# The state-space core of a hybrid mixer, placed between the units of the projection that follows it

## The chip, the core and the metric

The kernel runs on one core of one Trainium2 chip. The core has five engines that run their own queues of instructions: TensorE (PE; matrix products, results in the eight banks of PSUM), VectorE (DVE), ScalarE (ACT), GpSimd (POOL) and SyncE (SP, which here only issues transfers from HBM). They wait for each other by semaphores. The metric is the device time of one execution in microseconds (us), the median of several; lower is better. All data are float32.

## The reference, cut to what matters

Two transformer blocks run on 256 tokens of width 1024. The first block's mixer projects the normed tokens `h` with `w_in` and has two branches. The change touches the SSD branch's core and the GDN branch's projection, which are independent of each other until both outputs are concatenated:

```python
proj = h @ w_in
# GDN branch: 3072 columns q, k, v; 1024 columns gate z
qkv = silu(causal_dwconv(gdn_qkv, gdn_conv_w))          # 4 taps
q = l2norm(q_heads) * (128 ** -0.5); k = l2norm(k_heads)
o = gated_delta_rule_chunked(q, k, v, beta, g)          # the GDN core
gdn_out = rmsnorm(o, gdn_norm_g) * silu(gdn_z)
# SSD branch: xs (16 heads of 64), bm and cm (2 groups of 128), dt
xbc = silu(causal_dwconv(ssd_xbc, ssd_conv_w) + ssd_conv_b)
y = ssd_chunked(xs, dt, ssd_a_log, bm, cm) + ssd_d[:, None] * xs
y = y * silu(ssd_z)
ssd_out = rmsnorm(y.reshape(.., 2, 512), ssd_norm_g)
return concatenate([gdn_out, ssd_out], axis=-1) @ w_out
```

Behind the mixer come a mixture of 32 experts, and a second block with its own mixer and 32 experts.

## The kernel before

**Stages.** The program is a chain of `nc.Block()`s. In each block every engine has its own list of instructions, and at the end of a block all engines meet before the next begins. The blocks around the change are, in order: (1) modulation and first norm; (2) the SSD projection (three weight chunks for x, B, C, two for the gate, a narrow one for dt), with its convolution; (3) the SSD core; (4) the GDN projection; (5) the GDN core; (6) the late modulation, `w_out` and the router; then the experts.

**The ring of weights.** `ring` holds `SLOTS` = 6 slots of 4096 floats for each of 128 partitions, 2 MB each. Chunk n goes to slot n % 6. `load` (lines 168 to 180) runs on SP: it waits until the slot's previous chunk has been multiplied and starts the transfer. `take` makes TensorE wait for the arrival. The other large memory is `arena`, 25600 floats a partition, whose places are given out by hand for each block.

**Block 3, the SSD core** (lines 492 to 594) goes over the two token tiles t = 0, 1 of 128 tokens, and uses all eight banks of PSUM. For each tile ScalarE repeats the decays of 16 heads along 128 columns (`abc`, line 531), TensorE multiplies them by a triangle of ones (line 506; decay rows), and in the same go makes the group products and the transposes of B and x (lines 511 to 515). VectorE subtracts, giving exponents of 16 head matrices (line 554), ScalarE exponentiates them, VectorE copies B, C-B products and x out of PSUM and forms the operands (lines 559 to 569), TensorE multiplies them (line 519, 16 products of 64 columns; line 523 the state of tile 0, or line 525 the read of it in tile 1), and VectorE forms the output, its gate, its sum of squares and its norm (lines 577 to 594). Tile 1 needs the state of tile 0. Scratch lies in `arena`.

**Block 4, the GDN projection** (lines 614 to 686). The 24 units u are blocks of 128 output channels by 256 tokens, eight products of 256 columns each (line 635), written to PSUM bank u % 6. VectorE does the four taps of the convolution out of the bank (`conv`, lines 368 and 372), ScalarE the Silu (line 661), GpSimd the squares of the 16 units of q and k (line 624). From unit 16 on, one length product of 512 columns follows each unit (line 645; eight in all, in banks 6 and 7), copied out by ScalarE (line 665). Then come four gate units of 16 products of 512 columns (line 653), beside which ScalarE takes the logarithm and exponential of the lengths, and VectorE scales q and k.

**Block 5, the GDN core**: SP starts the transfer of the norm weight `gng` (line 731); VectorE's list begins with a wait for it (`dve.wait_ge(s_gn, 16)`), before its first operation (line 848).

**Order of the queues.** Nothing is reordered by a planner: an engine's list is the order in the source. `then_inc` raises a semaphore when an instruction is done, `wait_ge` holds the engine and all that is queued behind it. `vv(...)` is a VectorE instruction followed by a wait for its own end.

Of the kernel before, what the change touches and what calls it, by code (L numbers as in the profile page):

```python
# [11 lines left out]
P = 128  # L12
D = 1024
T = 2
# [27 lines left out]
def program(nc, a, out):  # L42
# [103 lines left out]
    class Ring:  # L146
# [3 lines left out]
        def __init__(self, name, slots=SLOTS):  # L150
            self.slots = slots
            self.full = [sem(f"{name}_slot{s}_full") for s in range(slots)]
            self.arrivals = []
            self.chunks, self.sent, self.used = [], 0, 0

        def add(self, src, shape, released):


            n = len(self.chunks)
            before = self.arrivals[n - self.slots] if n >= self.slots else 0  # L160
            self.arrivals.append(before + (32 if isinstance(src, list) else 16))
            self.chunks.append((src, shape, released))

        def last_uses(self):

            return [(n % self.slots, *self.chunks[n][2]) for n in range(len(self.chunks) - self.slots, len(self.chunks))]

        def load(self, sp, upto):
            while self.sent < min(upto, len(self.chunks)):
                n = self.sent  # L170
                src, (k, w), _ = self.chunks[n]
                s = n % self.slots
                if n >= self.slots:
                    sp.wait_ge(*self.chunks[n - self.slots][2])
                if isinstance(src, list):
                    for i in range(2):
                        sp.dma_start(slot(s, k, w)[64 * i:64 * i + 64], src[i]).then_inc(self.full[s], 16)
                else:
                    sp.dma_start(slot(s, k, w), src).then_inc(self.full[s], 16)
                self.sent += 1  # L180

        def take(self, pe):
            n = self.used
            pe.wait_ge(self.full[n % self.slots], self.arrivals[n])
            self.used += 1
            _, (k, w), _ = self.chunks[n]
            return slot(n % self.slots, k, w)
# [6 lines left out]
    for j in range(4):  # L194
        ra.add(cols(ada_w, 512 * j), (KD, 512), (s_ada, j + 1))
    for j in range(3):
        ra.add(cols(w_in, C_XBC + 512 * j), (KD, 512), (s_unit, 4 * j + 4))
    for j in range(2):
        ra.add(cols(w_in, C_SZ + 512 * j), (KD, 512), (s_unit, 12 + 2 * j + 2))
    for j in range(6):  # L200
        ra.add(cols(w_in, 512 * j), (KD, 512), (s_gunit, 4 * j + 4))
    for j in range(2):
        ra.add(cols(w_in, C_GZ + 512 * j), (KD, 512), (s_gunit, 24 + 2 * j + 2))
    for j in range(4, 12):
        ra.add(cols(ada_w, 512 * j), (KD, 512), (s_ada, j + 1))
    s_wout = sem("w_out_chunk_multiplied")
    for n in range(2):
        for k in range(2):
            ra.add(a["w_out"][0][1024 * k:1024 * k + 1024, 512 * n:512 * n + 512]
                   .rearrange("(k p) n -> p k n", p=P), (KD, 512), (s_wout, 2 * n + k + 1))  # L210
# [43 lines left out]
    with nc.Block() as block:  # L254
        @block.sync
        def _(sp):
# [14 lines left out]
            ra.load(sp, 4 + SLOTS)  # L271
# [89 lines left out]
    def conv(dve, n, nbanks, dst, tap0, bias0, ready, taken, taps):  # L361

        for u in range(n):
            dve.wait_ge(ready, u + 1)
            src = ps[:, u % nbanks, 0:T * P]
            w = [convw[:, tap0 + k * taps + u:tap0 + k * taps + u + 1] for k in range(4)]
            if bias0 is None:
                vv(V.tensor_scalar(dst(u), src, w[3], None, ALU.mult))
            else:
                vv(V.tensor_scalar(dst(u), src, w[3], convw[:, bias0 + u:bias0 + u + 1], ALU.mult, ALU.add))  # L370
            for s in (1, 2, 3):
                ins = V.scalar_tensor_tensor(dst(u)[:, s:T * P], src[:, 0:T * P - s], w[3 - s], dst(u)[:, s:T * P],
                                             ALU.mult, ALU.add)
                if s < 3:
                    vv(ins)
                else:
                    ins.then_inc(taken, 1)

    with nc.Block() as block:
        @block.sync  # L380
        def _(sp):
            ra.load(sp, 9 + SLOTS)
# [63 lines left out]
        def _(dve):  # L446
            conv(dve, 12, 8, lambda u: xbcT[:, u, :], 96, 144, s_unit, s_conv, 12)
# [15 lines left out]
    x_tok = ar(6400, D)  # L463
    b_tok = ar(7424, 2, P)
    xdt = ar(7680, D)
    xde = ar(8704, D)
    state = ar(9728, 2, 512)
    yb = ar(10752, D)
    abc = ar(17408, SH, P)
    dmat = ar(19456, SH, P)  # L470
    cbT = ar(21632, 2, P)
    ysq = ar(21888, D)
    sng = ar(22912, D)
# [3 lines left out]
    atot = small[:, 392:408]  # L477
# [5 lines left out]
    s_tr = sem("ssd_transposes")  # L483
# [5 lines left out]
    s_y3t = sem("ssd_products_taken")  # L489
    s_var3, s_root3 = sem("ssd_squares_summed"), sem("ssd_roots_ready")  # L490

    with nc.Block() as block:  # L492
        @block.sync
        def _(sp):
            sp.dma_start(sng, row_everywhere(a["ssd_norm_g"][0])).then_inc(s_p3, 16)

        @block.tensor
        def _(pe):
            for t in range(T):
                tok = slice(t * P, (t + 1) * P)  # L500
                pe.wait_ge(s_abc, t + 1)
                if t:
                    pe.wait_ge(s_y3t, 1)
                    pe.wait_ge(s_st, 1)
                for h in range(SH):
                    last = M.matmul(ps[:, h // 4, (h % 4) * P:(h % 4 + 1) * P], abc[:, h, :], tri_le[:, :])
                M.matmul(ps[:, 4, 0:SH], tri_le[:, :], dec[:, t, 8:24])
                last = M.matmul(ps[:, 4, 16:16 + SH], ones[:, :], dec[:, t, 8:24])
                last.then_inc(s_row, 1)
                for g in range(2):  # L510
                    M.matmul(ps[:, 5, g * P:(g + 1) * P], xbcT[:, 8 + g, tok], xbcT[:, 10 + g, tok])
                for g in range(2):
                    last = M.transpose(ps[:, 5, (2 + g) * P:(3 + g) * P], xbcT[:, 8 + g, tok], ident[:, :])
                for k in range(KD):
                    last = M.transpose(ps[:, 6 + k // 4, (k % 4) * P:(k % 4 + 1) * P], xbcT[:, k, tok], ident[:, :])
                last.then_inc(s_tr, 1)
                pe.wait_ge(s_m3, 2 * t + 2)
                for h in range(SH):
                    last = M.matmul(ps[:, h // 8, (h % 8) * SP_:(h % 8 + 1) * SP_], abc[:, h, :],
                                    xdt[:, h * SP_:(h + 1) * SP_])  # L520
                for g in range(2):
                    if t == 0:
                        last = M.matmul(ps[:, 2 + g, :], b_tok[:, g, :], xde[:, g * 512:(g + 1) * 512])
                    else:
                        last = M.matmul(ps[:, 2 + g, :], xbcT[:, 10 + g, tok], state[:, g, :])
                last.then_inc(s_y3, 2)

        @block.scalar
        def _(act):
            def repeat_decays(t):  # L530
                A.activation(abc, bcast(dec[:, t, 8:24], P), ACT.Copy).then_inc(s_abc, 1)
            repeat_decays(0)
            for t in range(T):
                act.wait_ge(s_dx, 3 * t + 1)
                A.activation(eac, acum, ACT.Exp).then_inc(s_de, 1)
                A.activation(edec, edec, ACT.Exp).then_inc(s_de, 1)
                for q in range(2):
                    act.wait_ge(s_dx, 3 * t + 2 + q)
                    A.activation(dmat[:, 8 * q:8 * q + 8, :], dmat[:, 8 * q:8 * q + 8, :], ACT.Exp).then_inc(s_de, 1)
                if t == 0:  # L540
                    act.wait_ge(s_y3, 2)
                    repeat_decays(1)
                    A.activation(state, banks(2, 2, 2, 512), ACT.Copy).then_inc(s_st, 1)
                act.wait_ge(s_var3, t + 1)
                A.activation(gss, gss, ACT.Sqrt, bias=eps_t, scale=1.0 / 512).then_inc(s_root3, 1)

        @block.vector
        def _(dve):
            for t in range(T):
                dve.wait_ge(s_row, t + 1)  # L550
                vv(V.tensor_copy(acum, ps[:, 4, 0:SH]))
                V.tensor_tensor(edec, ps[:, 4, 16:16 + SH], acum, ALU.subtract).then_inc(s_dx, 1)
                for h in range(SH):
                    ins = V.scalar_tensor_tensor(dmat[:, h, :], ps[:, h // 4, (h % 4) * P:(h % 4 + 1) * P],
                                                 acum[:, h:h + 1], neg_u, ALU.subtract, ALU.add)
                    if h % 8 == 7:
# [1983 lines left out]
```

## Time and profile before

| what | value |
|---|---|
| median of 3 runs | 2439.54 us (2438.66 to 2441.5) |
| profiled execution, its own time | 2437.12 us |
| its span | 2435.4 us |
| TensorE busy | 2124.4 us, 87% |
| VectorE, ScalarE, GpSimd busy | 569.1, 371.3, 82.0 us |
| granted TensorE clock, mean | 0.934 |

The span runs from the first to the last instruction of the profiled execution; 1.7 us of its own time lie outside. TensorE's busy time is that of its matrix products with modelled ends. The time before is the median; durations in the argument come from the one profiled execution.

### The profile page before, as it was taken

How to read it: one execution, taken by the hardware profiler on the slowest of the kernel's cores; microseconds unless marked ns; L12 is line 12 of the kernel's file. 1: busy time of each engine (PE TensorE's matmuls, PEld its weight loads, DVE VectorE, ACT ScalarE, POOL GpSimd, SP SyncE). 2: the span in 40 equal slices, each digit the busy share in tenths (PEclk: the TensorE clock that was granted, in tenths of full speed). 3: DMA queues.
4: the chain of work that ended last, by engine and by line, in shares of the span. 5: the costliest groups of instructions: out<-in, count | busy, mean ns of one | idle time of the engine just before them, and what ended most of it. 6: DMA issues, size and time to landing. Idle time of an engine off the chain costs nothing. (4 is left out here: it accounts for less than half of the span.)

```text
span 2435.4 us, 25005 instructions
## 1 busy us (share of the span) xinstructions
PE 2124.4 (87%) x10073; PEld 1099.0 (45%) x10073; DVE 569.1 (23%) x1204; ACT 371.3 (15%) x633; POOL 82.0 (3%) x151
## 2 busy tenths in 40 slices
PE   4957977796999999999999999699957699999997
PEld 1746846733444443333333333255544344444443
DVE  1345535413121111111111111322152300010001
ACT  2130132111000100000100000113230111111111
POOL 1000012200000000000000000100030000000000
PEclk7977988997899999999999999899958799999999
DMA  9511320093699999999999999734314179999995
GB/s 338 193 43 45 135 98 1 1 343 124 258 428 428 429 428 429 428 429 428 429 428 429 427 429 428 291 124 158 104 40 149 69 325 426 429 427 429 428 429 232
DMA packets 98733, 708.58 MB, mean 291 GB/s; under 512 B 12291, under 2 KB 17885, under 8 KB 61565
## 3 DMA queue, kind: packets, MB, share of 16 engines
q1 hardware_dynamic: 98684, 707.92, 70.9%
q8 instruction: 33, 0.54, 0.1%
q14 instruction: 16, 0.12, 0.0%
HBM read 706.85 MB, written 1.05 MB: 291 GB/s over the span
## 5 line engine op out<-in xcount | busy, mean ns | idle before, releaser
L1272 PE MATMUL ps<-ring,arena 128*64 128x512 f32 x2048 | 451.9, 594 | 28.1 <-DMA ring<-in_moe_w_gu 28.1
L1272 PEld LDWEIGHTS ps<-ring,arena 128*64 128x64 f32 x2048 | 161.3, 137 | 312.4 <-issue 247.9
L1294 PE MATMUL ps<-ring,arena 128*64 128x512 f32 x1024 | 226.8, 594 | 19.6 <-issue 19.6
L2401 PE MATMUL ps<-ring,arena 128*64 128x512 f32 x1024 | 224.9, 593 | 6.9 <-DMA ring<-in_w_up 5.4
L1294 PEld LDWEIGHTS ps<-ring,arena 128*64 128x64 f32 x1024 | 84.6, 137 | 141.2 <-issue 141.2
L2401 PEld LDWEIGHTS ps<-ring,arena 128*64 128x64 f32 x1024 | 78.2, 137 | 150.4 <-issue 150.4
L1609 PE MATMUL ps<-ring 128*128 128x512 f32 (+1 forms) x320 | 139.0, 586 | 1.2 <-DVE ring L1879 0.9
L2422 PE MATMUL ps<-ring,arena 128*64 128x512 f32 x512 | 113.4, 595 | 0.0
L1337 DVE TENSOR_SCALAR arena<-arena 128x256 f32<-128x256 f32 x33 | 11.7, 354 | 380.6 <-PE ps L1272 380.5
L1364 DVE TENSOR_SCALAR arena<-ps 128x512 f32<-128x512 f32 x32 | 22.1, 691 | 332.4 <-PE ps L1272 332.4
L1318 ACT ACTIVATE arena<-arena 128x512 f32<-128x512 f32 x32 | 20.2, 630 | 522.2 <-DVE arena L1364 522.2
L635 PE MATMUL ps<-arena,ring 128*128 128x256 f32 x384 | 86.4, 386 | 12.4 <-PEq L492 12.4
L1609 PEld LDWEIGHTS ps<-ring 128*128 128x128 f32 x320 | 60.3, 193 | 69.1 <-issue 66.2
L2461 DVE TENSOR_SCALAR arena<-iota_row,arena 128x64 f32<-128x64 f32 x68 | 12.6, 249 | 329.0 <-PE ps L2401 327.9
L635 PEld LDWEIGHTS ps<-arena,ring 128*128 128x128 f32 x384 | 74.4, 194 | 27.1 <-issue 17.0
L1235 PEld LDWEIGHTS ps<-arena 128*128 128x128 f32 x544 | 64.9, 196 | 27.5 <-issue 27.5
L1235 PE MATMUL ps<-arena 128*128 128x128 f32 x544 | 71.2, 286 | 0.0
L2379 PEld LDWEIGHTS ps<-arena 128*128 128x128 f32 x544 | 62.1, 192 | 13.5 <-issue 13.5
L1242 PE MATMUL ps<-arena 64*128 64x512 f32 x264 | 65.6, 615 | 0.8 <-ACT arena L1325 0.8
L2422 PEld LDWEIGHTS ps<-ring,arena 128*64 128x64 f32 x512 | 35.3, 137 | 66.7 <-issue 66.7
L2379 PE MATMUL ps<-arena 128*128 128x128 f32 x544 | 65.1, 278 | 0.0
L2386 PE MATMUL ps<-arena 128*128 128x512 f32 x136 | 61.3, 593 | 0.7 <-ACT arena L2454 0.7
(516 smaller groups left out, 2154.7 us busy)
## 6 DMA issues: line engine op xcount, KB each, us to landing
ring<-in_moe_w_gu SPq DMA_DIRECT2D x128, 2048.0 KB, 24.1
ring<-in_moe_w_down SPq DMA_DIRECT2D x64, 2048.0 KB, 21.4
ring<-in_w_down SPq DMA_DIRECT2D x32, 2048.0 KB, 12.2
ring<-in_w_gate SPq DMA_DIRECT2D x32, 2048.0 KB, 14.9
ring<-in_w_up SPq DMA_DIRECT2D x32, 2048.0 KB, 17.2
ring<-in_w_in SPq DMA_DIRECT2D x22, 2048.0 KB, 10.7
ring<-in_ada_w SPq DMA_DIRECT2D x12, 2048.0 KB, 9.5
ring<-in_w_out SPq DMA_DIRECT2D x6, 2048.0 KB, 19.2
```

The lines of the kernel that those rows point to most:

```text
L635: last = M.matmul(ps[:, u % 6, 0:T * P], w[:, k, c * P:(c + 1) * P], hT[:, k, :], start=(k == 0), stop=(k == KD - 1))
L1235: last = M.matmul(ps[:, bank, k4 * P:(k4 + 1) * P], x_tok[:, t, k * P:(k + 1) * P], onehot[:, t, :], start=(t == 0), stop=(t == T - 1))
L1242: last = M.matmul(ps[:, 2 * t + j, :], GT[halves[j], t, :], y2[halves[j], :], start=False, stop=False, skip_group_check=True)
L1272: last = M.matmul(ps[halves[j], 4 + which, :], xgT[buf][:, k, CAP * ee:CAP * ee + CAP], w[:, k2, at:at + 512], start=False, stop=(k == KD ...
L1294: last = M.matmul(ps[halves[j], 6, :], yT[:, k % KH, halves[k // KH]], w[:, k % KH, 512 * j:512 * j + 512], start=(k == 0), stop=(k == 2 * ...
L1318: A.activation(sg, tg, ACT.Sigmoid, scale=1.702).then_inc(s_sig, 1)
L1364: V.tensor_scalar(tg, ps[:, 4, :], 7.0, None, ALU.min).then_inc(s_g, 1)
L1609: last = M.matmul(ps[:, bank, 0:n], uT[:, k, t * P:(t + 1) * P], w[:, k, :], start=(k == 0), stop=(k == KD - 1))
L2379: last = M.matmul(ps[:, 6 + k // 4, (k % 4) * P:(k % 4 + 1) * P], x_tok[:, t, k * P:(k + 1) * P], onehot[:, t, :], start=(t == 0), stop=(t ...
L2386: M.matmul(ps[:, 2 * t + d, :], GT[:, t, :], y2[:, d, :], start=False, stop=False, skip_group_check=True)
L2401: last = M.matmul(ps[halves[j], 4 + which, :], xgT[:, k, halves[j]], w[j][:, k, :], start=(k == 0), stop=(k == KD - 1))
L2422: last = M.matmul(ps[halves[j], (4, 7)[d], :], yT[:, k, halves[j]], w[j][:, k, 512 * d:512 * (d + 1)], start=(k == 0), stop=(k == KH - 1))
```

## The change

Blocks 3 and 4 become one. Each step of the SSD core is a small function, and is called behind a given GDN unit, on each of the three engines that take part:

| behind unit (tile 0, tile 1) | TensorE | ScalarE | VectorE |
|---|---|---|---|
| 0, 8 | decay rows of heads 0 to 7, group products | exponentials of them | exponents of heads 0 to 7 |
| 1, 9 | | | B and C-B products taken |
| 2, 10 | decay rows of heads 8 to 15 | exponentials of them | exponents of heads 8 to 15 |
| 3, 11 | transposes of x | x taken | |
| 4, 12 | | | operands |
| 6, 14 | products | (6 only) decays repeated, state taken | outputs, gated |
| 7, 15 | | squares, root | norm |

Further parts of it:

- GDN units use `GB` = 3 banks (u % 3) and bank 3 takes the length products; banks 4 to 7 are the SSD core's, and later the gate units'.
- A length product follows every second unit from 5 to 19, not every unit from 16 to 23. It is copied out by ScalarE behind units 6, 8, ..., 20. Squares have four pairs of places (`sqT`), reused.
- x is taken out of PSUM by ScalarE, and the sums of squares of the output are made by ScalarE (`Square` with `accum_out`, two of 512 columns); VectorE did both.
- The SSD core's scratch lies in ring slots 3, 4 and 5. In this block the ring has only slots 0 to 2: each chunk now names its slot. Of the loads, chunks 12 to 16 (the last three of q, k, v and both gate chunks) are issued in the merged block, and the six chunks of `ada_w` that were issued in block 4 are issued at the start of block 5, behind `gng`. Chunk 9 is issued in block 2, no longer in block 1. In block 6 the last chunks and the experts' first loads have other slot numbers.

```diff
+    abc, dmat = slab(3, 0, SH, P), slab(3, 2048, SH, P)
+    x_tok, xdt, xde, state = slab(4, 0, D), slab(4, 1024, D), slab(4, 2048, D), slab(4, 3072, 2, 512)
+    yb, ysq = slab(5, 0, D), slab(5, 1024, D)
...
+    GB = 3
...
+            sp.dma_start(sng, row_everywhere(a["ssd_norm_g"][0])).then_inc(s_p3, 16)
+            ra.load(sp, 17)
...
+            def gdn_unit(u, w):
+                c = u % 4
+                if u >= GB:
+                    pe.wait_ge(s_gconv, u - GB + 1)
+                for k in range(KD):
+                    last = M.matmul(ps[:, u % GB, 0:T * P], w[:, k, c * P:(c + 1) * P], hT[:, k, :],
+                                    start=(k == 0), stop=(k == KD - 1))
+                last.then_inc(s_gunit, 1)
+
+            def lengths(b):
+                if b == 0:
+                    pe.wait_ge(s_on, 1)
+                else:
+                    pe.wait_ge(s_sqt, b)
+                pe.wait_ge(s_sq, 2 * b + 2)
+                M.matmul(ps[:, 3, :], ones128 if b < 4 else ones[:, :],
+                         sqT[:, b % 4, :, :].rearrange("p a b -> p (a b)")).then_inc(s_sqs, 1)
...
+            def decay_rows(t, q):
+                if q == 0:
+                    pe.wait_ge(s_abc, t + 1)
...
+                else:
+                    pe.wait_ge(s_dx, 3 * t + 2)
...
+            for u in range(24):
+                if u % 4 == 0:
+                    w = ra.take(pe)
+                gdn_unit(u, w)
+                if u in (0, 8):
+                    decay_rows(u // 8, 0)
+                    group_products(u // 8)
+                if u in (2, 10):
+                    decay_rows(u // 8, 1)
+                if u in (3, 11):
+                    value_transposes(u // 8)
+                if u in (6, 14):
+                    products(u // 8)
+                if u >= 5 and u % 2 == 1 and u <= 19:
+                    lengths((u - 5) // 2)
...
+            def squares(t):
+                act.wait_ge(s_yg, t + 1)
+                for g in range(2):
+                    A.activation(ysq[:, 512 * g:512 * g + 512], yb[:, 512 * g:512 * g + 512], ACT.Square,
+                                 accum_out=gss[:, g:g + 1]).then_inc(s_var3, 1)
+                act.wait_ge(s_var3, 2 * t + 2)
+                A.activation(gss, gss, ACT.Sqrt, bias=eps_t, scale=1.0 / 512).then_inc(s_root3, 1)
...
             for u in range(24):
                 act.wait_ge(s_gconv, u + 1)
                 A.activation(qkvT[:, u, :], qkvT[:, u, :], ACT.Silu).then_inc(s_gact, 1)
-                if u >= 16:
-                    b = u - 16
+                t = u // 8
+                if u in (0, 8):
+                    token_decays(t)
+                    pair_decays(t, 0)
+                if u in (2, 10):
+                    pair_decays(t, 1)
+                if u in (3, 11):
+                    take_values(t)
+                if u == 6:
+                    act.wait_ge(s_y3, 1)
+                    repeat_decays(1)
+                    A.activation(state, banks(4, 2, 2, 512), ACT.Copy).then_inc(s_st, 1)
+                if u in (7, 15):
+                    squares(t)
+                if u >= 6 and u % 2 == 0 and u <= 20:
+                    b = (u - 6) // 2
                     act.wait_ge(s_sqs, b + 1)
-                    A.activation(rsT[:, 2 * b:2 * b + 2, :], ps[:, 6 + b % 2, :].rearrange("p (a b) -> p a b", a=2),
+                    A.activation(rsT[:, 2 * b:2 * b + 2, :], ps[:, 3, :].rearrange("p (a b) -> p a b", a=2),
                                  ACT.Copy).then_inc(s_sqt, 1)
...
+            def outputs(t):
+                vv(V.tensor_tensor(sqh, xh, bcast(heads[:, 48:64], SP_), ALU.mult))
+                dve.wait_ge(s_y3, t + 1)
+                ins = V.tensor_tensor(yb, ysq, banks(6, 2, 1024), ALU.add)
...
+            def normed(t):
+                dve.wait_ge(s_root3, t + 1)
+                vv(V.reciprocal(gss, gss))
...
+            for u in range(24):
+                conv_unit(dve, u, GB, lambda v: qkvT[:, v, :], 0, None, s_gunit, s_gconv, 24)
+                t = u // 8
+                if u in (0, 8):
+                    pair_exponents(t, 0)
+                if u in (1, 9):
+                    take_groups(t)
+                if u in (2, 10):
+                    pair_exponents(t, 1)
+                if u in (4, 12):
+                    operands(t)
+                if u in (6, 14):
+                    outputs(t)
+                if u in (7, 15):
+                    normed(t)
...
             sp.dma_start(gng, row_everywhere(a["gdn_norm_g"][0])).then_inc(s_gn, 16)
+            ra.load(sp, 23)
```

## Rows read from the trace of the kernel before

**Rows 1.** The page: the span and TensorE in its 40 slices, tenths busy.

```profile
span 2435.4 us, 25005 instructions
...
PE   4957977796999999999999999699957699999997
```

**Rows 2.** Stages by windows, us: PE, PEld, DVE, ACT, POOL busy; PEclk, DMA share, GB/s.

```profile
130.50:135.98 5.48, 0.01 (x1) 0.00 (x0) 1.22 (x7) 3.49 (x6) 0.00 (x0) 0.70 0.68 259
135.98:210.24 74.26, 36.51 (x172) 31.12 (x172) 42.46 (x68) 15.33 (x18) 0.00 (x1) 0.64 0.02 7
210.24:330.74 120.50, 119.57 (x464) 89.61 (x464) 50.88 (x98) 28.89 (x44) 9.99 (x17) 0.98 0.36 123
```

**Rows 3.** Timeline of the SSD core's first tile, and of what follows it.

```profile
136.01 1.91 ACT L531 ACTIVATE arena<-small 128x2048 f32<-128x2048 f32 x1 [1.08 <-PEq L379]
...
137.97 6.17 PE L506 MATMUL ps<-tri_le,arena 128*128 128x128 f32 x32 [7.47 <-ACT arena L531]
...
144.83 4.22 DVE L554 SCALAR_TENSOR_TENSOR arena<-ps,small,masks 128x128 f32<-128x128 f32 x16
...
151.13 1.23 DVE L564 TENSOR_TENSOR arena<-arena,small 128x1024 f32<-128x1024 f32 x1
...
153.53 2.48 DVE L569 TENSOR_TENSOR arena<-arena 128x1024 f32<-128x1024 f32 x2
156.07 6.90 PEld L519 LDWEIGHTS ps<-arena 128*128 128x128 f32 x32 [10.18 <-DVE arena L569]
...
162.95 3.73 PE L523 MATMUL ps<-arena 128*128 128x512 f32 x4
...
167.97 1.22 DVE L578 TENSOR_TENSOR arena<-arena,ps 128x1024 f32<-128x1024 f32 x1
168.53 1.00 ACT L543 ACTIVATE arena<-ps 128x1024 f32<-128x1024 f32 x1
```

**Rows 4.** Timeline of the GDN projection: start, first units, one length product, gate units.

```profile
210.28 4.94 PE L635 MATMUL ps<-arena,ring 128*128 128x256 f32 x12 [12.37 <-PEq L492]
...
216.12 0.48 DVE L368 TENSOR_SCALAR arena<-ps,convw 128x256 f32<-128x256 f32 x1 [6.36 <-PE ps L635]
216.64 1.52 DVE L372 SCALAR_TENSOR_TENSOR arena<-ps,convw,arena 128x255 f32<-128x255 f32 x3
218.19 0.42 ACT L661 ACTIVATE arena<-arena 128x256 f32<-128x256 f32 x1 [6.67 <-DVE arena L372]
...
219.57 0.48 DVE L368 TENSOR_SCALAR arena<-ps,convw 128x256 f32<-128x256 f32 x1 [1.42 <-PE ps L635]
...
275.49 1.02 PE L645 MATMUL ps<-arena 128*128 128x512 f32 x2
...
302.21 27.63 PE L653 MATMUL ps<-ring,arena 128*128 128x512 f32 x64
```

**Rows 5.** Timeline of the GDN core's start: products of 128 columns, first VectorE operation.

```profile
333.91 0.37 PE L760 MATMUL ps<-small,ones 128*128 128x8 f32 x2
...
334.13 3.82 PE L752 MATMUL ps<-arena 128*128 128x128 f32 x32
337.81 0.17 DVE L848 COPY small<-ps 128x8 f32<-128x8 f32 x1 [20.20 <-DMA masks<-in_gdn_norm_g]
```

**Rows 6.** Windows of 2 us behind a pause of TensorE, columns as in rows 2.

```profile
170.00:172.00 2.00, 2.00 (x13) 2.00 (x12) 1.93 (x3) 0.83 (x1) 0.00 (x0) 0.55 0.03 8
172.00:174.00 2.00, 2.00 (x13) 2.00 (x13) 1.60 (x3) 0.98 (x2) 0.00 (x0) 0.60 0.00 0
```

**Rows 7.** Timeline: a table load and the activation behind it.

```profile
4.65 1.28 ACT L311 ACT_TABLE_LOAD   x1
5.95 0.21 ACT L311 ACTIVATE convw<-convw 128x8 f32<-128x8 f32 x1
```

More of the change, by code:

```diff
@@ L146, in program, with __init__, add @@
     class Ring:
[L150 to L162, printed above, removed]
+        def __init__(self, name):
+            self.full = [sem(f"{name}_slot{s}_full") for s in range(SLOTS)]
+            self.chunks, self.newest, self.sent, self.used = [], {}, 0, 0
+        def add(self, src, shape, released, s):
+            before = self.newest.get(s)
+            arrivals = 32 if isinstance(src, list) else 16
+            if before is not None:
+                arrivals += self.chunks[before][4]
+            self.newest[s] = len(self.chunks)
+            self.chunks.append((src, shape, released, s, arrivals, before))
         def last_uses(self):
-            return [(n % self.slots, *self.chunks[n][2]) for n in range(len(self.chunks) - self.slots, len(self.chunks))]
+            return [(s, *self.chunks[n][2]) for s, n in sorted(self.newest.items(), key=lambda item: item[1])]
         def load(self, sp, upto):
             while self.sent < min(upto, len(self.chunks)):
[L170 to L174, printed above, removed]
+                src, (k, w), _, s, _, before = self.chunks[self.sent]
+                if before is not None:
+                    sp.wait_ge(*self.chunks[before][2])
                 if isinstance(src, list):
@@ L446, in _ @@
         def _(dve):
-            conv(dve, 12, 8, lambda u: xbcT[:, u, :], 96, 144, s_unit, s_conv, 12)
+            for u in range(12):
+                conv_unit(dve, u, 8, lambda v: xbcT[:, v, :], 96, 144, s_unit, s_conv, 12)
             dve.wait_ge(s_unit, 18)
@@ new lines, in products @@
+            def products(t):
+                pe.wait_ge(s_m3, 2 * t + 2)
+                for h in range(SH):
+                    M.matmul(ps[:, 6 + h // 8, (h % 8) * SP_:(h % 8 + 1) * SP_], abc[:, h, :], xdt[:, h * SP_:(h + 1) * SP_])
+                for g in range(2):
+                    if t == 0:
+                        last = M.matmul(ps[:, 4 + g, :], b_tok[:, g, :], xde[:, g * 512:(g + 1) * 512])
+                    else:
+                        last = M.matmul(ps[:, 4 + g, :], xbcT[:, 10 + g, toks(t)], state[:, g, :])
+                last.then_inc(s_y3, 1)
@@ new lines, in _, with pair_exponents @@
+            sqh = ysq.rearrange("p (h q) -> p h q", h=SH)
+            def pair_exponents(t, q):
+                dve.wait_ge(s_row, 2 * t + q + 1)
+                if q == 0:
+                    vv(V.tensor_copy(acum, ps[:, 4, 0:SH]))
+                    V.tensor_tensor(edec, ps[:, 4, 16:16 + SH], acum, ALU.subtract).then_inc(s_dx, 1)
+                for h in range(8):
+                    ins = V.scalar_tensor_tensor(dmat[:, 8 * q + h, :], ps[:, 6 + h // 4, (h % 4) * P:(h % 4 + 1) * P],
+                                                 acum[:, 8 * q + h:8 * q + h + 1], neg_u, ALU.subtract, ALU.add)
+                ins.then_inc(s_dx, 1)
@@ L996, in load_first @@
         def load_first(self, sp, ring):
-            for s in range(ring.slots, SLOTS):
+            for s in sorted(set(range(SLOTS)) - set(ring.newest)):
                 src, k, w = self.chunks(0)[s]
@@ L1462, in add_z @@
     def add_z(j):
[L1463 removed]
+        rb2.add(cols(w2, 512 * j, z_width(j)), (KD, z_width(j)), (s_z, 2 * j + 2), len(rb2.chunks) % STREAM)
     for j in range(4):
```

298 lines of the change are left out of this document (117 added, 181 removed).

## The prediction

> **What bounds the kernel now.** I read the page first: TensorE is busy nine tenths and more in most slices of 61 us; the first ten, up to 609 us, are the first block's mixer and are mostly below that [rows 1]. Then the windows by stage, because the change lives in two of them. From 135.98 to 210.24 us, the SSD core, TensorE works 36.5 of 74.3 us, at a granted clock of 0.64, and VectorE 42.5: a chain that passes from engine to engine. From 210.24 to 330.74 us, the GDN projection, TensorE works 119.6 of 120.5 us at 0.98, VectorE only 50.9 and ScalarE 28.9 [rows 2]. So one stage waits for other engines, and the next has those engines more than half free. The timeline of the core shows the chain: TensorE's decay rows, 16 exponents on VectorE, operands on VectorE, and TensorE idle 10.18 us before its products [rows 3]. The timeline of the projection shows the pace: VectorE begins a convolution each 219.57 - 216.12 = 3.45 us and needs 0.48 + 1.52 + gap = 2.04 of them [rows 4]. What follows the mixer is a stream that starts when the mixer is done, so I count a shift of the mixer's end one for one: the experts' first weights can land long before routing is finished in either kernel, and nothing before it is due by the clock.
>
> **TensorE's list in the merged block, without waits.** It begins at 136.0 us instead of 210.28.
> - Units: the first ran at the low clock and took 216.12 - 210.28 = 5.84 less 0.2 for drain and signal, 5.65; 23 more at 3.45 are 79.35 [rows 4]. TensorE paused 5.5 us before 136.0, where the windows have the mean clock at 0.70 [rows 2], so the same slow start is right. 85.0.
> - Length products: one 512-column product is two passes of 27.63 / 64 = 0.43, so 0.86; eight are 6.9 [rows 4]. Gate units: 27.4 without the drain [rows 4].
> - SSD steps at full clock: 32 passes of 128 columns took 3.82 with the drain, 0.115 each [rows 5]. A half of the decay rows is 16 passes, 1.8; twice a tile. The two small products are 4 passes, 0.44; group products and B transposes 6 passes, 0.7; eight x transposes of one pass 0.92. The 16 products of 64 columns took 6.90 at the low clock [rows 3]. At the full clock no row shows them: below, 1.8 if they go by columns and clock; above, 6.9 if neither helps. I take 32 x 0.111 = 3.55, because their pace at the low clock, 0.216 a pass, is nearly twice the 128-column pace at full clock, so they seem to cost as much as those. Behind them two products of 512 columns, 1.72. In sum 10.95 a tile, 21.9.
> Together 85.0 + 6.9 + 27.4 + 21.9 = 141.2 us. If TensorE never waited, the block would end at 277.2 instead of 329.84: 52.6 us less.
>
> **Where TensorE waits.** I followed the three lists in order, with durations from rows 3 and 4 (Silu 0.42, exponents of 8 heads 2.1, exponential of 1024 columns 1.06, 1024-column VectorE step 1.25 with gap, table load 1.28). Most steps fit: a unit's bank is needed three units later, and VectorE's burst of operands (1.23 + 1.23 + 2.48) sits in front of two free units. Two places do not fit, both behind `normed`, one per tile.
> - Tile 0. Products end at 174.2. VectorE gates at about 176.9, waits for unit 7, and ends its convolution at 179.9. ScalarE's list has Silu of unit 7 first (180.4), then two squares (estimate 0.6 each, from 1.00 for 1024 columns and 1.91 for 2048 [rows 3]), a table load, the root: 183.2. VectorE has stood at `normed` since 179.9, with unit 8's convolution queued behind it; unit 8 was multiplied at 182.3. VectorE norms until 185.9, convolves 8 until 188.0, makes exponents until 190.4. Only then ScalarE's exponential and, behind it in its list, the copy of length 1 (192.1). TensorE reached length 2 at 188.7, which waits for that copy: 3.5 us. Late next is unit 10 and all behind it.
> - Tile 1. The same at unit 15: convolution ends 229.0, root 232.3, norm 235.1, convolution 16 at 237.1, Silu, copy of length 5 at 238.2. TensorE stands at length 6 since 233.0: 5.3 us.
> With 0.35 at length 1 TensorE waits 9.2 us. After a pause of 3.0 us (166.68 to 169.68 [rows 3]) the clock's mean was 0.55 and 0.60 in the next two windows of 2 us, and 1.0 would be full [rows 6]: low for about 3.4 us, 1.7 us lost. Both long waits are longer than that pause, so I add 1.75 each, 3.5 in all; below it is nothing. The Trainium skill, "TensorE: Matmul & The Clock Gate", section on HAM oscillation, warns against idle gaps between bursts of matmuls for this reason; the row agrees, and by the rule the price is the same.
> The end: 136.0 + 141.2 + 9.2 + 3.5 = 289.9, where it was 302.21 + 27.63 = 329.84 [rows 4]. **39.9 us less.**
>
> **Costs counted at nothing, with their cover.** Eight more table loads for exponentials and four for roots, 1.28 each = 15.4 us of ScalarE; all but the two roots' are covered, as ScalarE has under 50 us of work in 127, and the loads stand ahead of the waits in its list. Without cover a load is 1.28. GpSimd's squares run beside VectorE's steps, cover: a length product comes four units later; a port conflict could hold one VectorE step by one square, under 1 us. Loads: chunk 12 is issued at 156.8 and needed at 205, so 2 MB have 48 us. The six `ada_w` chunks move to the GDN core, which moves almost no data; they are needed 150 us later.
> Of a table load the row shows 1.28 us, and the next activation starts 0.02 later, at 5.95 [rows 7]. The Trainium skill, "ScalarE: Activation LUTs", section "What ACT_TABLE_LOAD costs", gives 1.28 plus a drain of 1.38, 2.66 for every switch. By that rule the lists end at 294.7, not 289.9; the row speaks against it.
>
> **A side effect.** In the GDN core VectorE's first step waited for the small `gng` transfer until 337.81, although its TensorE input was ready at 333.91 + 0.37 = 334.28 [rows 5]. The transfer had been queued 0.9 us behind a 2 MB `ada_w` chunk. After the change it goes ahead of the six. If it lands within 3.5 us of the block's start, VectorE starts 3.5 us earlier, and its chain leads this stage. Ends: 0 and 3.5; a loss is excluded as long as transfers land in the order of their issue, as `gng` did behind the chunk. I take 3.5, for it is 64 KB.
>
> **Sum.** 39.9 + 3.5 = 43.4. Against its own time, 2437.1 - 43.4 = 2393.7. The profiled execution is 2.4 us under the median of the runs, so I forecast **2396**.
>
> **Rivals.**
> 1. *TensorE hardly waits.* If the waits and the clock loss are not there, 2396 - 12.7 = 2383. For: they hang on ScalarE's order at two places. Against: both waits follow from lists without slack. Down to 2389 10%.
> 2. *A switch of tables holds ScalarE for about twice the load's 1.28.* The two roots then come 1.3 later and so do the Silus behind them; length copies 0, 1, 4 and 5 slip, TensorE waits 14 us instead of 9.2, and the time is 4.8 more: 2401. Against: the 0.02 us between load and activation [rows 7]. 6%. It is what the Trainium skill says in the section named above.
> 3. *Little is hidden.* VectorE has 36 us of SSD steps in the block (16.8 and 19.3 by tile), and it is in the path of banks, lengths and norm. If none is hidden TensorE takes 141.2 + 36, ends at 313.2, and with the 3.5 the time is 2419; half hidden gives 2401. For: three banks, one length bank. Against: 1.4 us of each 3.45 are free on VectorE, and a bank has three units. 2402 to 2425: 14%.
> 4. *Slower: the clock.* One mechanism: short waits between units keep TensorE at the low level, as in the core now (0.64 [rows 2]). Each microsecond at the low level costs half; 43.4 us are eaten when 87 us of the block's 154 are low, and from there on the kernel is slower. With the whole list low the block ends at 136 + 2 x 139 = 414, and the time is 2439.5 + 84 - 3.5 = 2520. For: TensorE's list gets a foreign step at ten places. Against: waits are short but for two, and in the GDN projection with lengths between units the clock stayed at 0.98. 4%.
> 5. *No gain:* a wait of 40 us that I don't see, a chunk of weights that arrives a block late for one. 2%.
>
> **How the numbers follow.** The forecast's own case, 2389 to 2402, has 64%, the rivals 10, 6, 14, 4 and 2. The range 2384 to 2412 takes rivals 1 and 2, the 64-column products at their upper end (+6.7), the side effect gone (+3.5), and half of rival 3; about 14% are left out. This kernel's measurement can't tell less than 0.2%, 4.9 us, from no change. Faster 94%, same 2%, slower 4%.
>
> **What would show it.** A gap at the first core's place is gone: TensorE over 90% busy from 136 to 290 us. The longest waits of TensorE there are the length products at units 9 and 17, 3.5 and 5.3 us, with the clock dipping behind each. The products of 64 columns take 3.5 us. VectorE's first step of the GDN core waits for TensorE, not for `gng`. Everything behind the mixer keeps its length. I am wrong if convolutions bunch up so that units wait for banks, if a chunk of weights is waited for, or if the clock stays below 1.0 between the steps.

## The result, and the profile after

The changed kernel takes 2396.32 us (median of 4 runs, 2391.07 to 2397.14), the kernel before 2439.2 in the same comparison. The ratio is 0.9818, 95% interval 0.9801 to 0.9835: 1.8% faster. The forecast was 2396, range 2384 to 2412.

The page of the kernel after, the same lines as [rows 1] and the clock:

```profile
span 2394.1 us, 25023 instructions
...
PE   4998977786999999999999999699858599999997
...
PEclk8999988996999999999999999899958799999999
```

The span is 41.3 us shorter (2435.4 before [rows 1]). The windows of the two stages behind the SSD projection, columns as in [rows 2]; the merged block first, then the GDN core:

```profile
133.70:289.65 155.95, 146.89 (x636) 111.87 (x636) 85.30 (x160) 58.74 (x79) 11.83 (x17) 0.95 0.20 71
289.65:446.55 156.90, 108.32 (x824) 103.32 (x824) 77.93 (x126) 31.90 (x45) 35.01 (x26) 0.87 0.22 81
```

The merged block takes 156.0 us where the two blocks took 74.3 + 120.5 [rows 2], and TensorE, which worked 156.1 of those 194.8, is busy 146.9 of 156.0. VectorE has 85 us of work in it instead of 93, ScalarE 59 instead of 44: the take of x, the squares, and eight table loads more (16 instead of 8). The parts of the 41.3 us, from the first transfer of each block: the merged block begins 2.3 us earlier (133.7, was 135.98), it is 38.8 shorter, the GDN core is 3.5 shorter (156.9, was 330.74 to 491.13, 160.4), and all that follows is 3.3 longer (1947.6 for 1944.3). Of the last, 1.9 us are scatter: the stretch from the first experts' start to the end is 1825.3 us here and 1823.4 before, and lay between 1820.3 and 1825.3 us in the profiles of the kernels with the change, with the same instructions in it. The other 1.4 us are in block 6 (122.3 for 120.9 us), whose first 7 us had a granted clock of 0.54 here and of 0.76 before; in nine profiles of kernels with the change block 6 took 122.3 us four times and 120.8 to 121.2 five times. The 3.5 us of the GDN core scatter too: with the norm weight issued in the same place it took 156.7 to 159.5 us in seven profiles.

What TensorE waited for in the merged block (us in total, times, longest):

```profile
PE ps L542 <- ACT arena L656: 8.1, 2, 4.9
PE ps L532 <- PEq L375: 5.5, 1, 5.5
```

Only the length products (line 542) wait, twice. The 5.5 is the meeting of the engines at the block's start. No unit's products wait for a bank, and no chunk of weights is waited for. The timeline of the first of the two waits:

```profile
175.83 0.30 PEld L542 LDWEIGHTS ps<-arena 128*128 128x128 f32 x2 [0.35 <-ACT arena L656]
...
179.65 1.28 ACT L633 ACT_TABLE_LOAD   x1
...
180.95 0.30 ACT L633 ACTIVATE small<-small 128x2 f32<-128x2 f32 x1
181.26 1.28 ACT L638 ACT_TABLE_LOAD   x1
...
182.74 1.23 DVE L723 TENSOR_TENSOR arena<-ring,small 128x1024 f32<-128x1024 f32 x1
...
184.00 0.48 DVE L364 TENSOR_SCALAR arena<-ps,convw 128x256 f32<-128x256 f32 x1
...
186.07 0.42 ACT L638 ACTIVATE arena<-arena 128x256 f32<-128x256 f32 x1 [3.52 <-DVE arena L368]
...
186.50 1.28 ACT L614 ACT_TABLE_LOAD   x1
...
188.42 1.06 ACT L619 ACTIVATE ring<-ring 128x1024 f32<-128x1024 f32 x1 [0.30 <-DVE ring L683]
...
189.38 0.58 ACT L656 ACTIVATE arena<-ps 128x512 f32<-128x512 f32 x1
...
190.01 1.95 PE L542 MATMUL ps<-arena 128*128 128x512 f32 x2 [3.25 <-ACT arena L656]
```

The first line is the length product before, of which only the weight load waits, 0.35 us. The others are to be read as one chain. ScalarE loads the root's table, takes the root and loads the Silu table; `normed` ends at 183.97; only then comes the convolution of unit 8 (184.00), though TensorE was through with that unit at about 180.3; then its Silu, the exponents, the exponential, and last the copy of a length (line 656) that TensorE's next length product waits for: 3.25 us. The second, at tile 1:

```profile
230.12 1.28 ACT L638 ACT_TABLE_LOAD   x1
...
235.25 0.58 ACT L656 ACTIVATE arena<-ps 128x512 f32<-128x512 f32 x1
...
235.88 2.07 PE L542 MATMUL ps<-arena,ones 128*128 128x512 f32 x2 [4.89 <-ACT arena L656]
```

4.89 us. Windows of 2 us behind both waits:

```profile
188.00:190.00 2.00, 0.00 (x0) 0.00 (x0) 1.89 (x6) 1.68 (x5) 0.00 (x0) 1.00 0.00 0
190.00:192.00 2.00, 1.99 (x3) 0.96 (x4) 1.09 (x3) 1.68 (x2) 0.23 (x1) 0.54 0.00 0
192.00:194.00 2.00, 2.00 (x7) 1.59 (x7) 0.00 (x0) 0.00 (x0) 0.38 (x1) 0.60 0.00 0
...
234.00:236.00 2.00, 0.12 (x1) 0.12 (x1) 1.89 (x5) 0.90 (x2) 0.00 (x0) 0.64 0.00 0
236.00:238.00 2.00, 2.00 (x3) 0.97 (x4) 0.80 (x2) 0.42 (x1) 0.00 (x0) 0.50 0.00 0
238.00:240.00 2.00, 2.00 (x6) 1.55 (x6) 0.00 (x0) 0.00 (x0) 0.00 (x0) 0.50 0.00 0
240.00:242.00 2.00, 2.00 (x8) 1.65 (x7) 0.00 (x0) 0.00 (x0) 0.00 (x0) 0.66 0.00 0
```

Worked out from these means, the clock behind the first is at its lower level for about 3.4 us, as it was behind the pause in [rows 6]. Behind the second it falls at about 234.6 and rises at about 241.4, so that TensorE works 5.5 us of it. And the first unit, the products of 64 columns, and the two of 512 behind them:

```profile
133.71 6.29 PE L532 MATMUL ps<-arena,ring 128*128 128x256 f32 x16 [5.53 <-PEq L375]
...
166.98 3.68 PE L575 MATMUL ps<-ring 128*128 128x64 f32 x32
...
170.50 1.94 PE L578 MATMUL ps<-ring,arena 128*128 128x512 f32 x4
```

### The profile page after: what moved, and what is told of

It is laid out like the page before. It is cut to its first block and busy times, and to the rows that moved or that the text cites. A ratio compares the mean times of both kernels' runs of the same rounds, so it can differ in the third digit from the quotient of the medians.

```text
span 2394.1 us, 25023 instructions
## 1 busy us (share of the span) xinstructions
PE 2115.1 (88%) x10073; PEld 1089.2 (45%) x10073; DVE 561.1 (23%) x1198; ACT 385.9 (16%) x651; POOL 83.4 (3%) x151
## 5 line engine op out<-in xcount | busy, mean ns | idle before, releaser
L1353 PEld LDWEIGHTS ps<-ring,arena 128*64 128x64 f32 x1024 | 84.5, 137 | 141.2 <-issue 141.2
## 6 DMA issues: line engine op xcount, KB each, us to landing
ring<-in_w_down SPq DMA_DIRECT2D x32, 2048.0 KB, 12.1
```

The lines of the kernel that those rows point to most:

```text
L1353: last = M.matmul(ps[halves[j], 6, :], yT[:, k % KH, halves[k // KH]], w[:, k % KH, 512 * j:512 * j + 512], start=(k == 0), stop=(k == 2 * ...
```

## The experiments

Each was run beside the kernel before, whose median was then 2436.6 to 2436.9 us; of the changed kernel, which was not run again, I use the 2396.3 above.

### Does the order on VectorE make the two waits?

```diff
-                if u in (7, 15):
-                    normed(t)
+                if u in (8, 16):
+                    normed(u // 8 - 1)
```

> The changed kernel with one edit: VectorE norms the SSD output behind unit 8 (tile 0) and unit 16 (tile 1), not behind 7 and 15, so that the convolution of the next unit is no longer queued behind the wait for ScalarE's root. Theory (the two long waits of TensorE come from that order): the same walk through the lists gives waits at length 2 of 0.3 us instead of 3.3, at length 6 of 1.8 instead of 4.9, no dip of the clock behind either, and the end of the merged block 10.3 us earlier; the time is 2386 where the changed kernel had 2396.3. Rival (the waits come from ScalarE's table loads and exponentials, or TensorE has another bound close behind): the waits stay over 2.5 us each and less than 4 us are won.

Measured: 2383.32 us (5 runs, 2382.64 to 2383.98), ratio 0.9778 (0.9765 to 0.9792). The waits of TensorE in the merged block:

```profile
PE ps L532 <- PEq L375: 5.5, 1, 5.5
PE ps L542 <- ACT arena L656: 1.4, 1, 1.4
```

and the block as one window, columns as above:

```profile
137.13:280.94 143.81, 141.48 (x636) 108.77 (x636) 85.45 (x160) 58.76 (x79) 11.85 (x17) 0.99 0.22 77
```

Of 3.25 and 4.89 us one wait of 1.4 is left, and the clock is at 0.99 over the block. The block is 143.8 us long instead of 156.0: 12.1 less, forecast 10.3. 6.7 of it are waits, and 4.4 are the two stretches at the lower clock level, half of the 3.4 and 5.5 us that TensorE worked in them. The last 1.0 is not the edit's. It lies in the first unit, ahead of every SSD step:

```profile
137.19 5.28 PE L532 MATMUL ps<-arena,ring 128*128 128x256 f32 x16 [5.52 <-PEq L375]
```

The same 16 passes took 6.29 us in the profile of the changed kernel, at a mean granted clock of 0.57 over 6.1 us, where here it was 0.73 over 6.0. The profiles of the kernels with 2 banks and with 1, with the squares on VectorE and with the copy first start like this one, so the changed kernel's block counts 1.0 shorter, 155.0, when theirs are compared with it. The medians say 13.0 us against the changed kernel, and 11.1 against the kernel with two banks below, which has the same two waits and ran in the same session. The rival is out.

### Are three banks tight?

```diff
-    GB = 3
+    GB = 2
```

> The changed kernel with two PSUM banks for the GDN units instead of three. Theory (no unit waits for a bank; VectorE's work is hidden in the gaps between units): nothing changes, 2396 within 0.2%, and TensorE waits for no convolution. Rival (rival 3 of the prediction: banks bind, and VectorE's steps reach TensorE through them): with one bank fewer TensorE waits for convolutions, over 5 us longer.

Measured: 2394.42 us (4 runs), ratio 0.9821 (0.9806 to 0.9836), the same as with three. TensorE's waits in the block:

```profile
PE ps L542 <- ACT arena L656: 8.1, 2, 4.9
PE ps L532 <- PEq L375: 5.5, 1, 5.5
```

The same two waits to 0.1 us, and none for a convolution. The block is 155.1 us long, for the 155.0 above. Rival 3 of the prediction, that VectorE's steps come through the banks, is refuted: there is a whole bank of slack. With one bank:

```diff
-    GB = 3
+    GB = 1
```

> The changed kernel with one PSUM bank for the GDN units. By the same walk through the lists TensorE now waits for nearly every convolution, 1.4 to 3.0 us each, 38 us in all instead of 9, and the merged block ends 27 to 29 us later: about 2424. If VectorE's latency mattered less than the walk says, it would be under 10 us later; if all of VectorE's 2.04 us and the signals of 23 units came on top of what is there, 47 us and more.

Measured: 2431.39 us, a single run. TensorE's waits:

```profile
PE ps L532 <- DVE arena L368: 32.6, 20, 2.9
PE ps L532 <- PEq L375: 5.5, 1, 5.5
PE ps L542 <- ACT arena L656: 0.2, 1, 0.2
```

20 waits for line 368, the last tap of a convolution, the longest 2.9 as expected, 32.6 us in all. The block is 190.0 us long, 34 more than with three as profiled, and the time 35 us longer; the walk had 27 to 29. Of the 34 the waits are 24.7 (32.8 for 8.1) and TensorE's own busy time 9.4 (156.3 for 146.9 us), which the walk did not have; what makes it is open. Direction and place are right, the sum is 5 to 8 us short.

### Is it the interleaving that gains?

The steps of both tiles stand in a loop of their own ahead of unit 0 on TensorE, ScalarE and VectorE; all else is as in the changed kernel:

```diff
+            for t in range(T):
+                decay_rows(t, 0)
+                group_products(t)
+                decay_rows(t, 1)
+                value_transposes(t)
+                products(t)
             for u in range(24):
                 if u % 4 == 0:
                     w = ra.take(pe)
                 gdn_unit(u, w)
```

> The changed kernel without the interleaving: one block, the same ring slots, scratch, banks, ScalarE squares and lengths formed as the units come, but all steps of both tiles stand in front of unit 0 on each engine. Theory (the gain is TensorE's idle time filled with units, and nothing else but the norm weight's earlier arrival): the core takes its 73 us again, the block ends near where it did before, the time is within 2430 to 2438. Rival (the lower number of VectorE operations, the ring's half or the missing barrier bring a good part): 2425 or less.

Measured: 2426.62 us (4 runs, 2426.05 to 2429.28), ratio 0.9959 (0.9943 to 0.9974). That is 10 us faster than before, 3.4 below my bounds and above the rival's 2425, so neither held. The changed kernel is 30 us faster still, and the kernel with two banks, run in the same session, 32: about three quarters of the gain need the interleaving. The timeline at the seam, which I had not thought through:

```profile
196.63 3.73 PE L580 MATMUL ps<-ring,arena 128*128 128x512 f32 x4
...
200.15 10.90 PE L532 MATMUL ps<-arena,ring 128*128 128x256 f32 x48
...
211.19 0.48 DVE L364 TENSOR_SCALAR arena<-ps,convw 128x256 f32<-128x256 f32 x1
...
213.28 12.31 PE L532 MATMUL ps<-arena,ring 128*128 128x256 f32 x48 [2.23 <-DVE arena L368]
```

Without a barrier TensorE starts unit 0 as soon as the products of tile 1 are multiplied, at 200.15. VectorE's ten microseconds of output and norm then lie beside the first three units; the fourth waits 2.2 us for a bank. From the block's start to unit 0 it is 66.5 us where it was 74.3 [rows 3, rows 4], and from there to the end 122.8 for 120.5. So the block is 189.3 us long, 5.4 less than the two before; the GDN core is 2.6 shorter, with the norm weight issued first.

### The norm weight of the GDN core

In the changed kernel the transfer is issued ahead of six others, and this is what came of it:

```profile
289.65 0.34 SPq L789 DMA_DIRECT2D masks<-in_gdn_norm_g  x1
...
292.82 0.37 PE L819 MATMUL ps<-small,ones 128*128 128x8 f32 x2
...
293.98 0.17 DVE L907 COPY small<-ps 128x8 f32<-128x8 f32 x1 [17.08 <-DMA masks<-in_gdn_norm_g]
```

It lands 4.3 us behind its issue, not within 3.5, so VectorE still waits for it, 0.8 us beyond TensorE's product, and starts 4.33 us into the block, where before it was 7.07. First the weight alone, in the kernel before, moved from the GDN core's block to the SSD core's, two blocks ahead:

```diff
             sp.dma_start(sng, row_everywhere(a["ssd_norm_g"][0])).then_inc(s_p3, 16)
+            sp.dma_start(gng, row_everywhere(a["gdn_norm_g"][0])).then_inc(s_gn, 16)
...
-            sp.dma_start(gng, row_everywhere(a["gdn_norm_g"][0])).then_inc(s_gn, 16)
+            pass
```

> The kernel before with the GDN norm weight's transfer moved to the SSD core's block, nothing else. Theory (the side effect is a part of the gain of its own): VectorE's first operation in the GDN core comes 3.5 us earlier, 3.6 behind the block's start and led by TensorE's product, and the GDN core is about 3.5 us shorter (160.4 before), the time some 3 us shorter. Rival (the chain has slack elsewhere): the operation comes earlier, and the stage is as long as it was.

Measured: 2433.82 us (11 runs), before 2436.85 (15 runs), ratio 0.9987 (0.9978 to 0.9996): 3.0 us. VectorE's first operation:

```profile
334.02 0.17 DVE L849 COPY small<-ps 128x8 f32<-128x8 f32 x1 [16.77 <-PE ps L761]
```

It now waits for TensorE and starts 3.6 us into the GDN core, where it was 7.1 in [rows 5]. The side effect is real on its own. Then the order turned round in the changed kernel, the weight behind the six chunks:

```diff
-            sp.dma_start(gng, row_everywhere(a["gdn_norm_g"][0])).then_inc(s_gn, 16)
             ra.load(sp, 23)
+            sp.dma_start(gng, row_everywhere(a["gdn_norm_g"][0])).then_inc(s_gn, 16)
```

> The changed kernel with the transfer of the GDN norm weight (64 KB) issued behind the six ada_w chunks at the start of the GDN core, not ahead of them. Theory (transfers land in the order of their issue, and this small one leads the core's chain): 12.6 MB at some 390 GB/s are ahead of it, it lands about 33 us after the block's start instead of 4.3, VectorE's first operation moves with it, and the time is 28 to 30 us longer, near 2425. Rival (the small transfer shares the engines with the large ones): it lands within 10 us and the time grows by under 6.

Measured: 2423.58 us, a single run, 27 longer. SyncE's issues (start, time until all are issued) and VectorE's first operation:

```profile
290.60 20.37 SPq L177 DMA_DIRECT2D ring<-in_ada_w  x6
311.00 5.62 SPq L790 DMA_DIRECT2D masks<-in_gdn_norm_g  x1
```

```profile
325.68 0.17 DVE L907 COPY small<-ps 128x8 f32<-128x8 f32 x1 [47.84 <-DMA masks<-in_gdn_norm_g]
```

The weight lands in the order of its issue, and VectorE starts 35.1 us into the block instead of 4.3. The GDN core is 187.7 us long instead of 156.9. So the place of one 64 KB transfer in one queue costs some 27 to 31 us here.

### Squares on ScalarE or on VectorE?

VectorE multiplies and sums again, ScalarE takes only the root:

```diff
-                V.tensor_tensor(yb, yb, mix[:, t, D:2 * D], ALU.mult).then_inc(s_yg, 1)
+                vv(V.tensor_tensor(yb, yb, mix[:, t, D:2 * D], ALU.mult))
+                vv(V.tensor_tensor(ysq, yb, yb, ALU.mult))
+                V.tensor_reduce(gss, ysq.rearrange("p (g n) -> p g n", g=2), X_AXIS, ALU.add).then_inc(s_var3, 1)
```

> The changed kernel with the output's squares and sums back on VectorE (two operations of 1024 columns a tile) and only the root on ScalarE. By the walk through the lists VectorE's own work grows by 2.5 us a tile and its wait for the root shrinks by 1.2; the waits at lengths 2 and 6 become 3.9 and 6.6 us where the walk has 3.5 and 5.3, and the block ends 1.6 us later: 2398, within the noise of 2396. Rival (moving the squares to ScalarE made the waits): 3 us or more are won.

Measured: 2396.22 us (4 runs), ratio 0.9834 (0.9816 to 0.9852). The two waits are 9.7 us together, the longest 6.2; the block is 157.4 us long, 1.5 more, or 2.5 against the 155.0. The four runs lie between 2391 and 2400 us, and nothing of it shows in their median. As expected: what this part of the change is worth in time is too small to be seen.

### The copy of the length ahead of the SSD steps

```diff
                 A.activation(qkvT[:, u, :], qkvT[:, u, :], ACT.Silu).then_inc(s_gact, 1)
+                if u >= 8 and u % 2 == 0 and u <= 20:
+                    b = (u - 6) // 2
+                    act.wait_ge(s_sqs, b + 1)
...
-                if u >= 6 and u % 2 == 0 and u <= 20:
+                if u == 6:
```

> The changed kernel with ScalarE's copy of each length moved ahead of the SSD steps of the same unit from unit 8 on (right behind its Silu). By the walk through the lists the wait at length 2 falls from 3.3 to about 0.5 us, because there the copy stood behind two small exponentials and one of 1024 columns; the wait at length 6 stays 4.9 to 5.3, because no exponential stands in front of that one. The block ends 4.8 us earlier with one dip of the clock less: 2391.5. Rival (only the order on VectorE matters): nothing changes.

Measured: 2389.82 us (5 runs, 2388.44 to 2390.23), ratio 0.9805 (0.9792 to 0.9819). The two waits:

```profile
187.62 1.13 PE L542 MATMUL ps<-arena 128*128 128x512 f32 x2 [0.26 <-ACT arena L642]
...
231.80 2.07 PE L542 MATMUL ps<-arena,ones 128*128 128x512 f32 x2 [4.90 <-ACT arena L642]
```

0.26 and 4.90: the one goes, the other stays, as the lists say. The block is 150.4 us long, 5.5 less: about 3.0 of wait, 1.7 of clock and the 1.0 of the first unit.

### SyncE and the end of the first block

The 2.3 us by which the merged block began earlier are no part of the prediction. ScalarE's last copy in the first block and its first instruction in the second, in the kernel before:

```profile
54.24 1.08 ACT L327 ACTIVATE arena<-ps 128x512 f32<-128x512 f32 x2 [1.31 <-PE ps L303]
...
56.15 1.28 ACT L434 ACT_TABLE_LOAD   x1 [0.82 <-PEq L254]
```

and in the kernel before with the norm weight moved, where ScalarE was done 1.7 us earlier and the second block began at the same time:

```profile
52.48 1.08 ACT L327 ACTIVATE arena<-ps 128x512 f32<-128x512 f32 x2 [1.31 <-PE ps L303]
...
56.16 1.28 ACT L434 ACT_TABLE_LOAD   x1 [2.59 <-PEq L254]
```

In both SyncE was issuing until 55.7 us, the last of six chunks being chunk 9, and the block's end waits for it; SyncE's issues in the kernel before (start, time until all are issued):

```profile
25.37 30.37 SPq L179 DMA_DIRECT2D ring<-in_w_in  x6
```

In the ten other profiles, nine of them of kernels with the change, the gap is 0.27 us. The part alone:

```diff
-            ra.load(sp, 4 + SLOTS)
+            ra.load(sp, 9)
```

> The kernel before with one edit: SyncE loads the ring only up to chunk 9 in the first block (chunks 0 to 8) and chunk 9 in the next block. Theory (a part of the gain that the prediction lacks: in both profiles of the kernel before, the first block ends at 56.15 us behind SyncE's issue of chunk 9 at 55.75, whether ScalarE was done at 55.3 or at 53.6; in all profiles with the change it ends 0.27 us behind ScalarE): the gap between ScalarE's last copy and the second block is 0.27 us, and the time 0.5 to 2 us shorter. Rival (that block's end is ScalarE's anyway, and its start differs by chance): the gap stays 0.5 us or more.

Measured: 2437.03 us (median of 11 runs), ratio 0.9996 (0.9987 to 1.0006). One of the 11 took 7775 us; why is not known, and it is left out of the ratio. The 0.5 to 2 us that I expected are not there. The profile:

```profile
55.03 1.08 ACT L327 ACTIVATE arena<-ps 128x512 f32<-128x512 f32 x2 [1.31 <-PE ps L303]
...
56.38 1.28 ACT L434 ACT_TABLE_LOAD   x1 [0.27 <-PEq L254]
```

The gap is gone, but ScalarE was done at 56.1 in this execution, so nothing is won in it, and none is shown in the median. The end of this block scatters from 54.1 to 56.6 us in the profiles with the change; SyncE's bound at 56.15 cuts in only where ScalarE is early. I claim no gain for it: 0.6 us of the 2.3 in the profiled pair are this gap, 1.6 are ScalarE's earlier end, which the other profiles show to be scatter.

### Both mends together

The changed kernel with `normed` behind units 8 and 16, and the norm weight issued in the merged block:

```diff
+            sp.dma_start(gng, row_everywhere(a["gdn_norm_g"][0])).then_inc(s_gn, 16)
...
-                if u in (7, 15):
-                    normed(t)
+                if u in (8, 16):
+                    normed(u // 8 - 1)
...
-            sp.dma_start(gng, row_everywhere(a["gdn_norm_g"][0])).then_inc(s_gn, 16)
```

> The changed kernel with both edits: norm one unit later, and the GDN norm weight loaded in the merged block. Theory: the first edit's 2383.3 less the 0.7 to 1.5 us by which the weight still holds VectorE's first operation (4.3 to 5.0 us behind the block's start where 3.6 is possible): 2382. If the clock in the GDN core falls otherwise, 2380 to 2385.

Measured: 2381.44 us (5 runs, 2380.75 to 2383.41), ratio 0.9776 (0.9763 to 0.979). It beats both kernels: 55 us under the one before, 15 under the changed one. VectorE starts 3.6 us into the GDN core.

## Why the prediction was right

**TensorE's list.** 141.2 us without waits was the main term. The 64-column products, whose price no row showed, took 166.98 to 170.50, 3.52 us; I had taken 3.55 between 1.8 and 6.9. The first unit took 6.1 us, not 5.65. From its first product to its last, TensorE needed 155.0 us in the merged block; I had 153.9. With 8.1 us of waits and 4.4 of clock taken off, the list itself was 142.5, 1.3 longer than mine, and the errors of the three terms (+1.3, -1.1, +0.9) partly cancel.

**Waits.** 3.25 and 4.89 us where I had 3.5 and 5.3. The 0.35 at length 1 is there too, but on the weight load alone (175.83); the products show no gap. That the two long ones come from the order of two lists, and not from banks, is shown three ways: `normed` one unit later takes the first and leaves 1.4 of the second (11.1 us with the clock), the copy ahead of the exponentials takes only the first, all but 0.26 (4.5 us with the clock), a bank less changes nothing.

**Clock.** Charged 3.5 us. The low stretches cost 1.7 behind the first wait and about 2.7 behind the second, 4.4, and removing the waits gave back as much, once the first unit's 1.0 is set aside. The mechanism was right, the size 0.9 too small: I had charged both waits with the same stretch, and the longer wait had a longer one.

**Table loads.** I counted twelve more and 15.4 us; there are eight more, 10.3 us, because the kernel before had loads of its own for exponentials and roots. ScalarE had 58.7 us of work in the block, not under 50. Neither moved the forecast. By the row, 1.28 and 0.02 us to the next activation; after: load from 179.65 to 180.93, root at 180.95. The Trainium skill ("ScalarE: Activation LUTs", "What ACT_TABLE_LOAD costs") adds a drain of 1.38; with it the waits would have come to 14 us, and they are 8.1. Rival 2 is out.

**Norm weight.** 3.5 us assumed, with landing within 3.5 us. It landed after 4.3, so VectorE won 2.7 in its start. The GDN core's length fell by 3.5 in this profile, and by 0.9 to 3.7 in the seven that issue the weight ahead of `ada_w`. The weight moved alone, in the kernel before, gave 3.0 in the median. By the 2.7 and the 3.0 the term was 0.5 to 0.8 too large, and that the profiled pair shows exactly 3.5 is luck.

**What made the sum agree.** In profiled spans: 38.8 for 39.9, 3.5 for 3.5, and a start 2.3 earlier against a rest 3.3 longer, neither forecast. Starts and rests of other profiles scatter as much. In medians 42.9 us for 43.4. Part of that closeness is luck: the median of the kernel before was 2439.2 to 2439.5 at first and 2436.6 to 2436.9 in later sessions, and against those the gain is 40.3 to 40.5.

**Rivals.** TensorE without waits (10%) was not what happened, but it is what the mended kernel reaches: 2381 for the 2383 given. Little hidden (14%) is refuted by the two banks. The clock at the lower level throughout (4%): the granted clock was 0.95 in the block. No gain (2%): no wait of that size is there.

## What to carry to other kernels

When a stage that waits stands next to one that keeps TensorE busy, write out TensorE's list and walk the other engines' lists beside it: the sum of the list gives the gain, and the walk finds the places, here two, where a copy that TensorE needs is queued behind a step that waits for another engine. Put such a step one unit later, behind the work that TensorE waits for; here that was worth 11 to 13 us beside the 40 to 43 of the whole change, for two lines. Look also at small transfers: the price of this one was its place in the queue, not its size. And before two profiles of a block are compared, compare a piece that both have in common, as the first unit here: it alone differed by 1.0 us.

## What the runs showed of the hardware that I had not expected

- The stretch at the lower clock level was longer behind the longer wait: about 3.4 us behind one of 3.25, about 6.8 around the end of one of 4.89, of which TensorE worked 5.5. In the kernel with the copy first a wait of 4.90 had again 6.8 us, of which TensorE worked 5.8.
- The first unit of the merged block, the same 16 passes behind the same 5.5 us of pause, took 6.3 to 6.5 us in three profiles and 5.2 to 5.3 us in five, as the granted clock rose later or earlier.
- A product of 64 columns costs nearly what one of 128 costs at the full level: the row of 32 passes is 3.68 us long at a granted clock of 1.00, where 32 passes of 128 columns have 3.82 in [rows 5].
- An issue can hold SyncE for microseconds: behind six chunks of 2 MB the issue of the 64 KB weight took it 5.62 us, where it took 0.34 ahead of them. In the first block of the kernel before the issue of one more chunk ended at 55.7 us, and the block's end at 56.15 waited for it in both profiles in which ScalarE was done earlier.
